# Third norm's mean square taken from sums of x·x, x·z and z·z collected during w_o, and the first FFN step on four tiles at once

## What is computed

```python
def rmsnorm(x, g):
    y = xf * lax.rsqrt(jnp.mean(xf * xf, axis=-1, keepdims=True) + EPS)
    return y * g
...
h = rmsnorm(x, pre_mix_g) * (1.0 + sc1) + sh1          # norm 1
y = hybrid_mixer(h, ...)                               # its last step is merged @ w_o
x = x + ga1 * rmsnorm(y, post_mix_g)                   # norm 2
h = rmsnorm(x, pre_ffn_g) * (1.0 + sc2) + sh2          # norm 3
y = swiglu_ffn(h, w_ffn_in, w_ffn_out)
```

## Time and profile before

| | |
|---|---|
| median of 3 runs | 1373.26 us (1372.94 to 1374.56) |
| the profiled execution's own time | 1375.59 us |
| its span, first to last instruction | 1373.9 us |
| mean granted TensorE clock | 0.996 of 2.4 GHz |
| busy: PE, DVE, ACT, POOL | 98%, 72%, 52%, 13% of the span |
| w_o ends, first result of its last tile taken | 375.0 us |
| first matmul of the first FFN | 393.3 us |
| last result of FFN tile 5 taken | 427.7 us |

### The profile page before, as it was taken

How to read it: one execution, slowest core, us unless ns; L and a number is a source line. 1 busy time by engine, 2 the same in 40 slices (tenths; PEclk the granted TensorE clock), 3 DMA queues, 4 the chain that set the end, 5 groups by cost and what they waited for, 6 DMA issues and landing times.

```text
span 1373.9 us, 19739 instructions
## 1 busy us (share of the span) xinstructions
PE 1346.9 (98%) x7756; PEld 1168.3 (85%) x7756; DVE 988.4 (72%) x1390; ACT 713.0 (52%) x1167; POOL 176.7 (13%) x165
## 2 busy tenths in 40 slices
PE   9999999999999999999999999999999999999997
PEld 6788888788769999998887778888778999998885
DVE  5889899778677787878425775667787888776332
ACT  3467787462465555564224443557565555564221
POOL 2479334200010000004000011121000000000000
PEclk9999999999999999999999999999999999999999
DMA  8523112456801233224522144543220323323221
GB/s 325 187 78 93 62 47 64 131 190 199 306 16 62 93 110 106 94 107 151 186 93 92 62 138 116 139 112 89 93 77 31 124 93 111 105 108 108 93 92 61
DMA packets 45309, 155.96 MB, mean 114 GB/s; under 512 B 6049, under 2 KB 6305, under 8 KB 45090
## 3 DMA queue, kind: packets, MB, share of 16 engines
q1 hardware_dynamic: 42882, 149.70, 32.6%
q0 software_dynamic: 2336, 5.01, 1.6%
...
## 4 chain that ended last, share of the span: by engine, by line
PE 87%; DVE 7%; ACT 3%; issue 1%; POOL 0%; DVEq 0%; ACTq 0%; POOLq 0%
PE ps L1758 26%; PE ps L1760 26%; PE ps L1759 26%; PE ps L1923 1%; DVE t_buf L1107 1%; DVE w_lo L1073 1%; PE ps L2189 1%; PE ps L1846 1%; ACT w_hi L584 1%; PE ps L1800 1%; PE ps L1858 1%; PE ps L1811 1%; PE ps L1812 1%; PE ps L1816 1%; DVE h_lo L1099 1%
## 5 line engine op out<-in xcount | busy, mean ns | idle before, releaser
L1758 PE MATMUL ps<-h_hi,w_hi 128*128 128x256 f32 (+1 forms) x1104 | 367.7, 333 | 4.2 <-DVE h_lo L1217 1.2
L1760 PE MATMUL ps<-h_hi,w_lo 128*128 128x256 f32 (+1 forms) x1104 | 365.3, 331 | 0.0
L1759 PE MATMUL ps<-h_lo,w_hi 128*128 128x256 f32 (+1 forms) x1104 | 365.3, 331 | 0.0
L1073 DVE TENSOR_TENSOR w_lo<-raw,w_hi 128x1024 fp32r<-128x1024 f32 x141 | 183.9, 1308 | 110.5 <-ACT w_hi L584 109.4
L1758 PEld LDWEIGHTS ps<-h_hi,w_hi 128*128 128x128 f32 x1104 | 209.8, 190 | 27.6 <-issue 4.9
L1760 PEld LDWEIGHTS ps<-h_hi,w_lo 128*128 128x128 f32 x1104 | 209.8, 190 | 19.8
L1759 PEld LDWEIGHTS ps<-h_lo,w_hi 128*128 128x128 f32 x1104 | 209.9, 190 | 18.9 <-issue 0.5
L584 ACT ACTIVATE w_hi<-raw 128x1024 fp32r<-128x1024 f32 x141 | 148.1, 1055 | 140.2 <-PE ps L1760 69.9
L1063 DVE TENSOR_TENSOR w_lo<-quads,w_hi 128x1024 fp32r<-128x1024 f32 (+1 forms) x152 | 165.0, 1086 | 72.6 <-ACT w_hi L584 72.6
L584 ACT ACTIVATE w_hi<-quads 128x1024 fp32r<-128x1024 f32 (+1 forms) x152 | 144.3, 950 | 78.3 <-PE ps L1760 76.6
L1758 PE MATMUL ps<-act_hi,w_hi 128*128 128x512 f32 x352 | 137.0, 389 | 0.0
...
## 6 DMA issues: line engine op xcount, KB each, us to landing
quads<-in_ffn_in SPq DMA_DIRECT2D x76, 512.0 KB, 4.4
raw<-in_ffn_out SPq DMA_DIRECT2D x44, 512.0 KB, 3.7
raw<-in_ada SPq DMA_DIRECT2D x32, 512.0 KB, 4.3
raw<-in_qk SPq DMA_DIRECT2D x25, 512.0 KB, 3.7
ada<-in_ada SPq DMA_DIRECT2D x16, 512.0 KB, 7.2
raw<-in_gates SPq DMA_DIRECT2D x16, 512.0 KB, 3.7
raw<-in_v SPq DMA_DIRECT2D x12, 512.0 KB, 3.7
raw<-in_ffn_in SPq DMA_DIRECT2D x12, 512.0 KB, 3.9
```

Of the source, the lines that this page charges most:

```text
L1073: nc.vector.tensor_tensor(w_lo[SLOT[p]][:], raw[q % RAW][:], w_hi[SLOT[p]][:].bitcast(f32), ALU.subtract).then_inc(raw_used, 1)
L1758: nc.tensor.matmul(out, w[0], v[0], start=start, stop=False, **kw)
L1759: nc.tensor.matmul(out, w[0], v[1], start=False, stop=False, **kw)
L1760: return nc.tensor.matmul(out, w[1], v[0], start=False, stop=stop, **kw)
```

## The change

- While w_o runs, ScalarE makes three results per tile in place of two: the square of y, z = y · g into `y_mix`, and z² into `sq_z`. So g is worked out before w_o, at the start of the merge.
- x is loaded again during w_o (before panel 3), not during the first FFN panels. GpSimd multiplies x and z and adds the products up in `acc_xz` for tiles 0 to 6; VectorE adds z² up in `acc_z`, and makes the last x·z itself.
- The sum of x² of norm 1 is kept (`ms_x`, one more copy by ScalarE at the start of the kernel) and brought into PSUM by a matmul with the identity, after w_o tiles 0 and 1. The two other terms are added there by two more such matmuls.
- r, r² and a third factor come from one Ln by three Exps. The table is loaded before the last result of w_o.
- GpSimd adds all 8 tiles of norm 2 to x. VectorE scales tile k+2 of z between making t of tile k and h_lo of tile k-1, and t is in PSUM (`T_BANK`).
- The first FFN starts with `many_tiles` on tiles 0 to 3: of each tile of h first all products with h_hi, then all with h_lo. Its panels 0 and 1 have buffers of their own (`ASIDE`), so that panels 0 to 3 are prepared during w_o. The sums of token halves move behind the halves of the panel of tile 4.
- `pair_in(0, 0)` moves to panel 7 of w_o. The semaphores of both FFNs are merged.

```diff
-ASIDE = {FIRST["qk2"] + 2: (0, FIRST["ffn_out1"] + 21), FIRST["qk2"] + 3: (1, FIRST["ffn_out1"] + 21)}
+ASIDE = {FIRST["qk2"] + 2: (0, FIRST["ffn_out1"] + 21), FIRST["qk2"] + 3: (1, FIRST["ffn_out1"] + 21),
+         FIRST["ffn_in1"]: (2, FIRST["merge"] + KT), FIRST["ffn_in1"] + 1: (3, FIRST["merge"] + KT)}
+AT_ONCE = 4
...
-                if (name, i) == ("wo", 5):
+                if (name, i) == ("wo", 7):
                     pair_in(0, 0)
-                if (name, i) == ("ffn_in1", 1):
+                if (name, i) == ("wo", 3):
                     sp.wait_ge(mg_c, KT)
                     sp.dma_start(x[:], t["x"]).then_inc(x_again, 16)
...
             pool.wait_ge(x_again, 16)
-            for k in range(0, KT, 2):
+            for m in range(KT - 1):
+                pool.wait_ge(y_out["wo"], m + 1)
+                if m == 0:
+                    nc.gpsimd.tensor_tensor(acc_xz[:], x[:, m, :], y_mix[:, m, :], ALU.mult).then_inc(xz_sum, 1)
+                    continue
+                pool.wait_ge(xz_sum, 2 * m - 1)
+                nc.gpsimd.tensor_tensor(xz[:], x[:, m, :], y_mix[:, m, :], ALU.mult).then_inc(xz_sum, 1)
+                pool.wait_ge(xz_sum, 2 * m)
+                nc.gpsimd.tensor_tensor(acc_xz[:], acc_xz[:], xz[:], ALU.add).then_inc(xz_sum, 1)
+            pool.wait_ge(xz_end, 1)
+            for k in range(KT):
                 pool.wait_ge(yt_ready, k + 1)
-                nc.gpsimd.tensor_tensor(x[:, k, :], x[:, k, :], t_buf[k // 2 % 2][:], ALU.add).then_inc(x_even, 1)
...
+            nc.scalar.activation(ms_x[:], ps[:, MS_BANK[1], :], ACT.Copy)
...
+            for m in range(KT):
+                prepare("wo", (0, 1, 2, 3, 4, 6, 7, 9)[m])
+                if m == KT - 1:
+                    tables(LN_EXP_TABLES)
                 used("wo", m)
-            y_tiles("wo", 1, lambda m: WO_BANK[m % 4], y_mix, wo_last)
-            tables(LN_EXP_TABLES)
-            root(2, ps[:, ROOT_2, :])
-            for k in range(KT):
-                act.wait_ge(*(x_ready, k // 2 + 1) if k % 2 else (x_even, k // 2 + 1))
-                square(2 * KT + k, sq[k % 2][:], x[:, k, :])
-            root(3)
-            h_halves(1, lambda k: mod[:, 24 + k:25 + k], keep=True)
+                y, g = ps[:, WO_BANK[m % 4], :], gain[:, 1, m:m + 1]
+                if m >= 2:
+                    act.wait_ge(sq_used, m - 1)
+                    act.wait_ge(zz_used, m - 1)
+                nc.scalar.activation(sq[m % 2][:], y, ACT.Square).then_inc(sq_ready, 1)
+                nc.scalar.activation(y_mix[:, m, :], y, ACT.Copy, scale=g).then_inc(y_out["wo"], 1)
+                nc.scalar.activation(sq_z[m % 2][:], y, ACT.Square, scale=g).then_inc(zz_ready, 1)
+            root(2, sq[1][:])
+            nc.scalar.activation(sq[0][:], rstd[:], ACT.Exp, scale=-1.0).then_inc(r2_powers, 1)
+            nc.scalar.activation(ps[:, ROOT_2, :], rstd[:], ACT.Exp, scale=-0.5).then_inc(r2_powers, 1)
+            act.wait_ge(r2_powers, 2)
+            act.wait_ge(x2_sums, 3)
+            nc.scalar.activation(rstd[:], ps[:, MS_BANK[3], :], ACT.Ln, bias=eps[:]).then_inc(ms_log, 1)
+            act.wait_ge(ms_log, 3)
+            nc.scalar.activation(ps[:, ROOT_3, :], rstd[:], ACT.Exp, scale=-0.5).then_inc(rstd_ready, 1)
+            h_halves(1, lambda k: mod[:, 24 + k:25 + k], keep=True, t_of=lambda k: ps[:, T_BANK[k % 2], :])
...
+            def norms_2_and_3():
 
                 def scaled(k):
-                    if k >= 4 and k % 2 == 0:
-                        dve.wait_ge(x_even, k // 2 - 1)
-                    if k >= 3 and k % 2:
-                        dve.wait_ge(x_ready, k // 2)
-                    nc.vector.scalar_tensor_tensor(out=ps[:, ODD_2, :] if k % 2 else t_buf[k // 2 % 2][:],
-                                                   in0=y_mix[:, k, :], scalar=gain[:, 1, k:k + 1],
-                                                   in1=ps[:, ROOT_2, :], op0=ALU.mult, op1=ALU.mult)\
+                    nc.vector.tensor_tensor(y_mix[:, k, :], y_mix[:, k, :], ps[:, ROOT_2, :], ALU.mult)\
                         .then_inc(yt_ready, 1)
+
+                def lo(k):
+                    dve.wait_ge(th_ready, H_AT[1] + k + 1)
+                    dve.wait_ge(hf_ready, k + 1)
+                    nc.vector.scalar_tensor_tensor(out=h_lo[:, k, :], in0=ps[:, T_BANK[k % 2], :],
+                                                   scalar=mod[:, 24 + k:25 + k], in1=h_hi[:, k, :].bitcast(f32),
+                                                   op0=ALU.add, op1=ALU.subtract).then_inc(h_ready, 1)
                 dve.wait_ge(rstd_ready, 2)
+                dve.wait_ge(x2_sums, 1)
+                nc.vector.scalar_tensor_tensor(out=t_buf[0][:], in0=ps[:, XZ, :], scalar=2.0, in1=sq[1][:],
+                                               op0=ALU.mult, op1=ALU.mult).then_inc(x2_terms, 1)
+                dve.wait_ge(r2_powers, 1)
+                dve.wait_ge(x2_sums, 2)
+                nc.vector.tensor_tensor(t_buf[1][:], ps[:, ZZ, :], sq[0][:], ALU.mult).then_inc(x2_terms, 1)
+                dve.wait_ge(r2_powers, 2)
                 scaled(0)
                 scaled(1)
-                for k in range(1, KT, 2):
-                    if k + 1 < KT:
-                        scaled(k + 1)
-                    dve.wait_ge(yt_ready, k + 1)
-                    nc.vector.tensor_tensor(x[:, k, :], x[:, k, :], ps[:, ODD_2, :], ALU.add).then_inc(x_ready, 1)
+                dve.wait_ge(rstd_ready, 3)
+                for k in range(KT):
+                    dve.wait_ge(x_even, k + 1)
+                    if k >= 2:
+                        dve.wait_ge(h_ready, H_AT[1] + k - 1)
+                    nc.vector.scalar_tensor_tensor(out=ps[:, T_BANK[k % 2], :], in0=x[:, k, :],
+                                                   scalar=gain[:, 2, k:k + 1], in1=ps[:, ROOT_3, :], op0=ALU.mult,
+                                                   op1=ALU.mult).then_inc(t_ready, 1)
                     if k + 2 < KT:
                         scaled(k + 2)
+                    if k:
+                        lo(k - 1)
+                lo(KT - 1)
...
+            def add_zz(m):
+                dve.wait_ge(zz_ready, m + 1)
+                if m:
+                    dve.wait_ge(zz_used, m)
+                nc.vector.tensor_tensor(acc_z[:], acc_z[:], sq_z[m % 2][:], ALU.add).then_inc(zz_used, 1)
             for m in range(KT):
-                feed("wo", m, dots=m < 3)
+                feed("wo", (0, 1, 2, 3, 4, 6, 7, 8)[m], dots=m < 3 or m == 4)
                 if m < KT - 1:
-                    add_square(KT + m)
+                    add_square(m)
+                    add_zz(m)
                 if m == 6:
                     first_sums(0, 0)
                     second_sums(0, 0)
+            dve.wait_ge(x_again, 16)
+            dve.wait_ge(y_out["wo"], KT)
+            z = y_mix[:, KT - 1, :]
+            nc.vector.tensor_tensor(xz_last[:], z, x[:, KT - 1, :], ALU.mult).then_inc(xz_end, 1)
+            add_zz(KT - 1)
+            feed("wo", KT + AT_ONCE - 1 - AHEAD)
...
+                if s == 0:
+                    feed(name, AT_ONCE - AHEAD)
+                    first_token_sums()
+                    second_token_sums()
+                    for n in range(3):
+                        sum_lo(n)
+                    feed(name, AT_ONCE + 1 - AHEAD)
...
+            nc.tensor.matmul(ps[:, MS_BANK[3], :], ident[:], ms_x[:], start=True, stop=False)
...
-            sum_over_features(2)
+            pe.wait_ge(sq_used, KT - 1)
+            nc.tensor.matmul(ps[:, MS_BANK[2], :], ones_d[:], acc[:], start=True, stop=False)
+            pe.wait_ge(sq_ready, KT)
+            nc.tensor.matmul(ps[:, MS_BANK[2], :], ones_d[:], sq[1][:], start=False, stop=True).then_inc(sq_used, 1)
+            pe.wait_ge(xz_sum, 2 * KT - 3)
+            nc.tensor.matmul(ps[:, XZ, :], ones_d[:], acc_xz[:], start=True, stop=False)
+            pe.wait_ge(xz_end, 1)
+            nc.tensor.matmul(ps[:, XZ, :], ones_d[:], xz_last[:], start=False, stop=True).then_inc(x2_sums, 1)
+            pe.wait_ge(zz_used, KT)
+            nc.tensor.matmul(ps[:, ZZ, :], ones_d[:], acc_z[:], start=True, stop=True).then_inc(x2_sums, 1)
+            pe.wait_ge(y_out["wo"], KT)
             pe.wait_ge(ms_log, 2)
-            busy(1, 4)
+            busy(REST, 4)
             pe.wait_ge(rstd_ready, 2)
-            busy(1, 4)
-            pe.wait_ge(yt_ready, 1)
-            busy(1, 4)
-            sum_squares(3)
-            after_sums(3, 1)
+            busy(REST, 4)
+            pe.wait_ge(x2_terms, 1)
+            nc.tensor.matmul(ps[:, MS_BANK[3], :], ident[:], t_buf[0][:], start=False, stop=False)
+            busy(REST, 2)
+            pe.wait_ge(x2_terms, 2)
+            nc.tensor.matmul(ps[:, MS_BANK[3], :], ident[:], t_buf[1][:], start=False, stop=True).then_inc(x2_sums, 1)
+            busy(REST, 4)
+            pe.wait_ge(ms_log, 3)
+            busy(REST, 5)
```

(11 more changed lines are left out.)

144 lines of the change are left out of this document (81 added, 63 removed).

## The result

The changed kernel takes 1377.69 us in the median of its 8 runs (1376.23 to 1379.06), the kernel before 1373.19 in 8 runs beside them: a ratio of 1.003, 95% interval 1.0021 to 1.0038. It is 4.5 us slower, or 0.3%, and the interval does not reach 1. The forecast was 1373.4, no difference, with a range up to 1377.2; the measured time is 0.5 us above that.

The account below looks back on a forecast made before the run. TensorE, busy 98% of the span, bounds the kernel; the change attacks an 18.3 us chain before the first FFN. -0.4 at tile 5's end and +0.5 at the start give +0.1: 1375.7 profiled, 1373.4 median, range 1367.4 to 1377.2.

Parts of the forecast that it names:

- Start, +0.5: Kernel start: ScalarE's copy of norm 1's sum delays the first matmul, unhidden, by 0.5 us (0.3 to 0.6).
- Price of a GpSimd instruction, 1.05: In w_o, VectorE and GpSimd take turns; each GpSimd instruction costs a fully loaded VectorE 1.05 us.
- the rival in which GpSimd loses them: In w_o, GpSimd loses the turns, VectorE's queue is 13.6 us shorter: 1367.5 us; chance 0.30, wholly or in half.
- The other rival's price: In w_o, a GpSimd instruction costs VectorE its whole length, 1.26 us: 2.7 us more, 1376.2 us; chance 0.10.
- TensorE's own tiles are in time: In w_o, the lo half of panel 7 is there at 368.3, two us before its tile.
- The queue to the dot behind panel 6: VectorE in w_o from 342.4: 14.1 us of own work, 9.5 for GpSimd; dot ends at 366.0 instead of 361.1.
- it lands 3.9 us later: Load of FFN panel 0 during w_o: lands 3.9 us after its buffer is free, near 369.8.
- The queue behind the hi half of panel 0: VectorE from 370.9: 11.1 us of work and 4.2 for four GpSimd instructions; first new term starts at 386.2.
- The tail: From first term at 386.2 through terms, Ln at 391.1 and 14 fillers to the first FFN matmul at 394.5.
- the third rival: TensorE's clock falls to 0.50 between 376 and 394, middle +3 us in all: 1376.4 us; chance 0.15.
- -0.4 at the end of tile 5: First FFN, last matmul of tile 5: 427.2 against 427.6 before, so 0.4 us earlier, start copy not counted.
- Behind it nothing changes: TensorE is busy throughout: After the first FFN's tile 5, the rest of the kernel neither gains nor loses time.

Follow-up runs that it names:

- no_xz: Changed kernel without the products x*z and their sums of w_o tiles 1 to 6 on GpSimd; 1367.06 us, 0.996 of the kernel before.
- sums_psum: Changed kernel with VectorE's two running sums in w_o kept in PSUM until their last addition; 1372.13 us, 0.9986 of the kernel before.

## Why the prediction was wrong

Here are its own steps, with its times turned into distances from Ln (19.66 in the profile that it read), and its start copy of 0.5 included:

- *Start, +0.5*: right. Ln to the first matmul took 3.53 us, 3.10 before: +0.43.
- *Price of a GpSimd instruction, 1.05*: right, 1.08. That the two engines take turns was the correct mechanism; the rival in which GpSimd loses them would have given 369.5, which is what the kernel without GpSimd work shows. The other rival's price, the whole length of 1.26, is above what was measured.
- *"TensorE's own tiles are in time"*: not quite. TensorE waited for the lo half of w_o panel 4 at 353.18 (0.29 us idle) and was held up again at 358.87 behind that of panel 5. The last matmul of w_o starts 357.10 us after Ln, 356.25 in the kernel without GpSimd work. The 0.8 is hidden, since TensorE then waits 4.54 us for VectorE anyway.
- *The queue to the dot behind panel 6*: forecast 346.8 for the load of FFN panel 0, measured 347.6 (365.55 less 17.95). 0.8 late, of which 0.6 is idle time of VectorE behind its first and second sum, while it waited for z² and for a hi half of ScalarE; the sum had it busy throughout.
- *"it lands 3.9 us later"*: mis-sized. The hi half starts 4.76 us after the issue of its load. The 3.9 was the median of twelve loads in the whole kernel; this one took 4.7, and 5.2 in no_xz and 4.6 in sums_psum. The unit quads of `pair_in(0, 1)`, which the prediction saw in the way, are not the cause: they are issued at 368.97, behind most of it, and in the two other kernels just as the load lands. What makes it longer stays open. 0.9 late.
- *The queue behind the hi half of panel 0*: forecast 15.3 us from there to the first term; measured 386.91 less 371.37, 15.5. Right; another 0.2.
- *The tail*: forecast 8.3 us from the first term to the first FFN matmul, measured 8.66. The two sets of fillers were in the forecast; that they were worth removing, 2.3 us, it didn't say. 0.4 late.
- *The FFN in 32.65 us*: 32.96 from the first matmul (395.57) to ScalarE's hi half behind tile 5 (428.53), 34.36 before. No wait inside it. It gives 1.4 us.
- *The clock*: the fall between 376 and 394 came as the third rival had it, and as its row of the kernel's start suggested. But "the middle +3 in all" was wrong: it is hidden but for 0.3 us at most, since VectorE's first term is later than the slow sums. What costs 1.5 us in the profile is a second fall, at a stretch of the code that the change didn't touch. That elsewhere behind the start the clock is 1.00 the prediction took from a row of w_o alone.

So the step that failed is the sum's "-0.4 at the end of tile 5": it was +2.1 beside the start copy, because the queue and its tail were mis-sized, by 0.8 up to the issue of the load of FFN panel 0, 0.9 in that load, and 0.2, 0.4 and 0.3 behind it. And "Behind it nothing changes: TensorE is busy throughout" is the step that failed for the other 1.5: 567.50 us from the head stage to the last Ln in place of 565.96. Why the clock falls there stays open. Both are small against a sum that set 9.9 us of removed work (a table load of 1.28, sums of 7.7, h_lo of 0.9) against as much of new queue; 2.4 us to either side of the likeliest case was too narrow for that.
